# A transformer block in split fp32 on one Trainium2 core: dense passes read from the last token to the first, operands placed at other distances from the weights

## The reference, cut to what matters

```python
h = rms_norm(x, norm1_g); z = h @ w_in            # first block: four mixers on slices of z
x = x + mix @ w_out
hf = causal_dwconv(rms_norm(x, norm2_g) @ w_up, ffn_conv_w, ffn_conv_b)
gt, val = split(hf); x = x + (gelu(gt) * val) @ w_down
x = x + (p @ w_pe) * sigmoid(rms_norm(x, norm3_g) @ w_pg)
for l in range(2):                                 # second block, twice
    proj = (rms(x) * norm1_g) @ w_in               # attention, RWKV-7, retention, gates
    x = x + (g0 * o_a + g1 * o_b + g2 * o_c) @ w_out
    h2 = rms(x) * norm2_g
    x = x + (silu(h2 @ w_gate) * (h2 @ w_up)) @ w_down
```

## Time and profile before

| | |
|---|---|
| median of 3 runs | 2564.78 us |
| the profiled execution, its own time | 2564.04 us |
| its span, first to last instruction | 2562.2 us |
| TensorE busy | 2528.5 us, 99% of the span, 16344 matmuls |
| TensorE weight loads | 2012.7 us, 79% |
| GpSimd busy | 1510.1 us, 59% |
| VectorE busy | 1311.9 us, 51% |
| ScalarE busy | 691.3 us, 27% |
| mean granted TensorE clock | 0.998 of full |

### The profile page before, as it was taken

The page is one execution under the profiler, slowest core; times in us unless marked ns, Lnnn a source line. Parts: engine busy times, 40 slices in busy tenths (PEclk is TensorE's granted clock), DMA queues, the critical chain, the costliest instruction groups (busy, mean ns, idle before and its releaser), DMA issues.

```text
span 2562.2 us, 47105 instructions
## 1 busy us (share of the span) xinstructions
PE 2528.5 (99%) x16344; PEld 2012.7 (79%) x16344; DVE 1311.9 (51%) x1979; ACT 691.3 (27%) x1290; POOL 1510.1 (59%) x963
## 2 busy tenths in 40 slices
PE   8989999999999999999999999999999999999999
PEld 6868888887877778888888888877778888888887
DVE  7866555455566657763322224566547663322224
ACT  4452000034134446522100002135446521100002
POOL 5666666655646455556666666646455556666665
PEclk9999999999999999999999999999999999999999
DMA  4213222223211132223222223211132223222222
GB/s 166 71 46 115 94 95 98 92 84 116 98 44 52 43 100 73 72 79 103 99 93 96 98 92 120 91 51 52 43 98 71 69 85 103 92 97 98 91 97 99
DMA packets 72442, 222.55 MB, mean 87 GB/s; under 512 B 9312, under 2 KB 12256, under 8 KB 72288
## 3 DMA queue, kind: packets, MB, share of 16 engines
q1 hardware_dynamic: 71856, 220.36, 26.0%
q10 hardware_dynamic: 432, 0.14, 0.0%
HBM read 218.37 MB, written 2.10 MB: 86 GB/s over the span
## 4 chain that ended last, share of the span: by engine, by line
PE 93%; DVE 3%; DVEq 1%; DMA 1%; issue 1%; POOL 1%; ACT 0%; ACTq 0%; POOLq 0%; SPq 0%
PE acc L547 81%; PE bank L547 10%; DMA raw<-in_w_pg 1%; PE bank L1213 0%; POOL w_lo L377 0%; DVE y_lo L1251 0%; DVE sumsq L1251 0%; POOL w_hi L370 0%; DMA vec<-in_vec 0%; DVE xg_lo L1344 0%; DVE att L1463 0%; DVEq L1411 0%; DVEq L1708 0%; DVEq L1464 0%; DVE rw_kp L1732 0%
## 5 line engine op out<-in xcount | busy, mean ns | idle before, releaser
L377 POOL TENSOR_TENSOR w_lo<-raw,w_hi 128x1024 fp32r<-128x1024 f32 (+3 forms) x438 | 962.8, 2198 | 308.5 <-PE acc L547 246.0
L370 POOL TENSOR_SCALAR w_hi<-raw 128x1024 fp32r<-128x1024 f32 (+3 forms) x438 | 434.9, 993 | 596.1 <-PE acc L547 511.5
L547 PE MATMUL acc<-xg_hi,w_hi 128*128 128x512 f32 x2208 | 582.7, 398 | 6.1 <-DVE xg_lo L1344 3.2
L547 PE MATMUL acc<-xg_lo,w_hi 128*128 128x512 f32 x2208 | 569.0, 393 | 0.0
L547 PE MATMUL acc<-xg_hi,w_lo 128*128 128x512 f32 x2208 | 562.6, 393 | 0.2 <-POOL w_lo L377 0.2
L547 PEld LDWEIGHTS acc<-xg_hi,w_hi 128*128 128x128 f32 x2208 | 408.6, 188 | 107.6 <-issue 20.1
L547 PEld LDWEIGHTS acc<-xg_hi,w_lo 128*128 128x128 f32 x2208 | 411.4, 188 | 88.3 <-issue 1.5
L547 PEld LDWEIGHTS acc<-xg_lo,w_hi 128*128 128x128 f32 x2208 | 411.4, 188 | 87.5 <-issue 1.5
L2130 ACT ACTIVATE ffn_act<-ffn_t 128x512 f32<-128x512 f32 x100 | 63.3, 633 | 748.4 <-DVEq L1311 605.7
L1251 DVE TENSOR_TENSOR x<-x,acc 128x512 f32<-128x512 f32 x104 | 71.5, 688 | 323.5 <-PE acc L547 322.9
L1251 DVE TENSOR_TENSOR bank<-acc,rstd 128x512 f32<-128x512 f32 x72 | 50.4, 699 | 263.4 <-PE acc L547 263.2
(11 more groups left out here) (351 smaller groups left out, 2710.8 us busy)
## 6 DMA issues: line engine op xcount, KB each, us to landing
raw<-in_w_up SPq DMA_DIRECT2D x132, 512.0 KB, 3.2
raw<-in_w_down SPq DMA_DIRECT2D x48, 512.0 KB, 3.2
raw<-in_w_gate SPq DMA_DIRECT2D x48, 512.0 KB, 3.2
raw<-in_w_ret SPq DMA_DIRECT2D x32, 512.0 KB, 3.2
raw<-in_w_rw SPq DMA_DIRECT2D x28, 512.0 KB, 3.2
raw<-in_w_o SPq DMA_DIRECT2D x48, 256.0 KB, 2.7
raw<-in_w_in SPq DMA_DIRECT2D x18, 512.0 KB, 3.3
raw<-in_w_down SPq DMA_DIRECT2D x24, 384.0 KB, 3.0
```

Of the source, the lines that this page charges most:

```text
L370: nc.gpsimd.tensor_scalar(w_hi[:, s, 0:n], raw[:, s, 0:n], 1.0, 0.0, ALU.mult, ALU.add).then_inc(w_half[s], 1)
L377: nc.gpsimd.tensor_tensor(w_lo[:, s, 0:n], raw[:, s, 0:n], bits(w_hi[:, s, 0:n]), ALU.subtract).then_inc(w_split[s], 1)
L547: return nc.tensor.matmul(o, a, b, start=first, stop=last, skip_group_check=shared)
```

## The change

Every dense pass goes through a new helper `dense`, which hands `mm` its moving operand and its PSUM output with the token dimension reversed, both with step -1. Token t still meets output column t, and the weights are read as before. A helper `columns_of` names the weight slice. The small matmuls of the mixers, the norm sums (`stats`) and the transposes stay with `mm`.

The layout changes: `xg` stays at remainder 128 and the weights stay at 128. `raw` moves from 160 to 128, `rstd`, `sumsq` and what follows them by 32 bytes. The first block's `y` goes from 480 to 128, `emb` from 192 to 128, `z_rw` (whose space `y1` and `z_at` share) from 256 to 384. `z_rt` (whose space `y2` and `hid` share) stays at 256. So, with the weights at 128, the moving operands stand at distances 0 (`xg`, `y`, `emb`), 256 (`y1`) and 128 (`y2`, `hid`), where they were at 0 (`xg`), 352 (`y`), 64 (`emb`) and 128 (`y1`, `y2`, `hid`).

```diff
-WEIGHTS, OTHERS = 128, 160
+PLACE, PLACE_B1, PLACE_RT = 128, 384, 256
...
-        xg_hi, _ = place("xg_hi", (DC, T), F32R)
-        xg_lo, _ = place("xg_lo", (DC, T), F32R)
+        xg_hi, _ = place("xg_hi", (DC, T), F32R, line=PLACE)
+        xg_lo, _ = place("xg_lo", (DC, T), F32R, line=PLACE)
...
-        raw, _ = place("raw", (2, DC * P))
-        w_hi, _ = place("w_hi", (2, DC * P), F32R, line=WEIGHTS)
-        w_lo, _ = place("w_lo", (2, DC * P), F32R, line=WEIGHTS)
-        rstd, _ = place("rstd", (T,), line=OTHERS)
+        raw, _ = place("raw", (2, DC * P), line=PLACE)
+        w_hi, _ = place("w_hi", (2, DC * P), F32R)
+        w_lo, _ = place("w_lo", (2, DC * P), F32R)
+        rstd, _ = place("rstd", (T,))
...
-        y_hi, _ = place("y_hi", (DC, T), F32R)
-        y_lo, _ = place("y_lo", (DC, T), F32R)
+        y_hi, _ = place("y_hi", (DC, T), F32R, line=PLACE)
+        y_lo, _ = place("y_lo", (DC, T), F32R, line=PLACE)
...
-        z_rw, rw_at = place("z_rw", (14, T))
-        z_rt, rt_at = place("z_rt", (16, T))
+        z_rw, rw_at = place("z_rw", (14, T), line=PLACE_B1)
+        z_rt, rt_at = place("z_rt", (16, T), line=PLACE_RT)
...
-        emb_at = base + 24 * 1024
+        emb_at = base + 24 * 1024 + (PLACE - base) % LINE
...
+            def columns_of(w, s, k):
+
+                return w[:, s, k * P:(k + 1) * P]
...
+            def dense(o, a, b, first, last, shared=False):
+
+                return mm(o[:, ::-1], a, b[:, ::-1], first, last, shared)
...
                     for k, c in enumerate(chunks):
-                        last = mm(o[:], w[:, s, k * P:(k + 1) * P], v[:, c, :], v is hi and m == 0 and k == 0, m == 1 and k == n - 1)
+                        last = dense(o[:], columns_of(w, s, k), v[:, c, :], v is hi and m == 0 and k == 0, m == 1 and k == n - 1)
```

More of the change, by code:

```diff
@@ L582, in late @@
                     for k, c in enumerate(chunks[:-1]):
-                        w = slice(k * P, (k + 1) * P)
                         pe.wait_ge(ready, count + k + 1)
                         pe.sem_inc(pe_turn, 1)
-                        mm(acc[s][:], w_hi[:, s, w], a[0][:, c, :], k == 0, False)
-                        mm(acc[s][:], w_hi[:, s, w], a[1][:, c, :], False, False)
+                        dense(acc[s][:], columns_of(w_hi, s, k), a[0][:, c, :], k == 0, False)
+                        dense(acc[s][:], columns_of(w_hi, s, k), a[1][:, c, :], False, False)
                     pe.wait_ge(w_split[s], I + 2)
@@ L590, in late @@
                     for k, c in enumerate(chunks[:-1]):
-                        mm(acc[s][:], w_lo[:, s, k * P:(k + 1) * P], a[0][:, c, :], False, False)
+                        dense(acc[s][:], columns_of(w_lo, s, k), a[0][:, c, :], False, False)
                     if stat is not None:
@@ L595, in late @@
                     pe.sem_inc(pe_turn, 1)
[L596 to L599, removed]
+                    k, c = n - 1, chunks[-1]
+                    dense(acc[s][:], columns_of(w_hi, s, k), a[0][:, c, :], False, False)
+                    dense(acc[s][:], columns_of(w_hi, s, k), a[1][:, c, :], False, False).then_inc(hi_done[s], 1)
+                    dense(acc[s][:], columns_of(w_lo, s, k), a[0][:, c, :], False, True).then_inc(slot_done[s], 1)
                     return
                 for i, k in enumerate(order or range(n)):
-                    w, c = slice(k * P, (k + 1) * P), chunks[k]
+                    c = chunks[k]
                     pe.wait_ge(ready, count + i + 1)
                     pe.sem_inc(pe_turn, 1)
-                    mm(acc[s][:], w_hi[:, s, w], a[0][:, c, :], i == 0, False)
-                    last_hi = mm(acc[s][:], w_hi[:, s, w], a[1][:, c, :], False, False)
-                    last = mm(acc[s][:], w_lo[:, s, w], a[0][:, c, :], False, i == n - 1)
+                    dense(acc[s][:], columns_of(w_hi, s, k), a[0][:, c, :], i == 0, False)
+                    last_hi = dense(acc[s][:], columns_of(w_hi, s, k), a[1][:, c, :], False, False)
+                    last = dense(acc[s][:], columns_of(w_lo, s, k), a[0][:, c, :], False, i == n - 1)
                 last_hi.then_inc(hi_done[s], 1)
@@ L618, in three @@
             def three(s, a, k, first, last):
[L620 to L623, removed]
+                dense(acc[s][:], columns_of(w_hi, s, k), a[0][:, k, :], first, False)
+                hi_pass = dense(acc[s][:], columns_of(w_hi, s, k), a[1][:, k, :], False, False)
+                return hi_pass, dense(acc[s][:], columns_of(w_lo, s, k), a[0][:, k, :], False, last)
             def hid_slots(I, n, count, ahead=0):
@@ L815, in _ @@
             for c in full:
-                w = w_hi[:, 0, c * P:(c + 1) * P]
-                mm(acc[0][:], w, xg_hi[:, c, :], c == 0, False)
-                last = mm(acc[0][:], w, xg_lo[:, c, :], False, False)
+                w = columns_of(w_hi, 0, c)
+                dense(acc[0][:], w, xg_hi[:, c, :], c == 0, False)
+                last = dense(acc[0][:], w, xg_lo[:, c, :], False, False)
             last.then_inc(hi_done[0], 1)
@@ L821, in _ @@
             for c in full:
-                last = mm(acc[0][:], w_lo[:, 0, c * P:(c + 1) * P], xg_hi[:, c, :], False, c == DC - 1)
+                last = dense(acc[0][:], columns_of(w_lo, 0, c), xg_hi[:, c, :], False, c == DC - 1)
                 if c < DC - 1:
@@ L832, in one @@
                 def one(s, w, v, c, first=False, last=False):
-                    return mm(acc[s][:], w[:, s, c * P:(c + 1) * P], v[:, c, :], first, last, True)
+                    return dense(acc[s][:], columns_of(w, s, c), v[:, c, :], first, last, True)
                 def started(s):
@@ L887, in part @@
                         w, v, c = (w_hi, w_hi, w_lo)[k // DC], (xg_hi, xg_lo, xg_hi)[k // DC], k % DC
-                        last = mm(acc[s][:], w[:, s, c * P:(c + 1) * P], v[:, c, :], k == 0, k == 3 * DC - 1, True)
+                        last = dense(acc[s][:], columns_of(w, s, c), v[:, c, :], k == 0, k == 3 * DC - 1, True)
                         if k == 2 * DC - 1:
```

## The result

| | before | after |
|---|---|---|
| median | 2564.41 us (4 runs) | 2603.12 us (4 runs, 2601.37 to 2603.97) |
| ratio, 95% interval | | 1.015 [1.0132, 1.0168] |
| span of the profiled execution | 2562.2 us | 2600.8 us |
| TensorE busy | 2528.5 us | 2571.2 us |

The change makes the kernel slower by 38.7 us. The forecast was 2499 us.

A forecast was written before the change was run, and what follows sets the result against it. TensorE was taken to bound the kernel, its dense passes lengthened by two SBUF streams meeting. Savings of 36.0 + 2.3 + 18.6 + 7.7 = 64.6 us from 2564.0 us gave 2499 us, range 2445 to 2605.

The forecast's parts named there:

- step 3: Dense passes' PSUM output: writing the accumulator backwards costs 0 ns a pass.
- R3: Rival: the reversed PSUM write is slow, 429 ns a pass, about 4475 us in all; chance 0.03.
- I take half of each excess as gone: All dense passes: reversing the moving operand removes half the time above 214.5 ns, 6.1 ns per `xg` pass, 9.45 per `hid`.
- the prediction's floor of 214.5 ns: Dense pass with nothing in its way, read from the fp32 record as two streams of 512 columns, 214.5 ns each.
- the term of `xg`: `xg` passes, 6.1 ns less each: 36.0 us saved outside the RWKV gaps and 2.3 us as filler.
- R2: Rival: distance 0 suits forward order only; reversed `xg` loses 6.7 ns a pass, 2609 us, or 2627 with others; chance 0.22.
- R1: Rival: `xg`'s 12.2 ns excess is a fixed cost per fp32r pass, whatever the order; 2545 or 2564 us; chance 0.25.
- Step 2: New distances: first block's `y` and `emb` at 0 gain 1.6 us forward, `y1` at 256 between -2.5 us and 0.
- The filler: 768 `xg` passes in the RWKV stretches: 4.7 us saved, half counted, 2.3 us, since shorter filler partly becomes longer waits.

The follow-up runs named there:

- scan_quiet: Dense passes alone, no block computed; read and write reversed separately at 64 distances: at distance 0, 226.7 ns a pass read forward, 233.3 read reversed.
- the scans: Three kernels of dense passes alone, no block computed, varying reading order, distance, address and columns; 331 to 763 us.
- step 0: In a kernel of dense passes alone, the moving operand reads one value over and over: 215.7 to 215.9 ns a pass at all eight distances.
- zero_fwd: Kernel after the change, but read forward and with every moving operand at distance 0 from the weights: 2547.45 us, ratio 0.9932 to before.

## Why the prediction was wrong

**The frame held.** TensorE bounds the kernel, a pass's time from start to start is the quantity, and its change shows in the time: the spans differ by 38.6 us, the sums of starts by the same. No other engine came in, the 32-byte moves cost nothing that shows, and the backward write is free, as costed in step 3; R3 fell by scan_quiet.

**The step that failed** is the first, "I take half of each excess as gone". It took 6.1 ns off each `xg` pass and 9.45 off each `hid` pass. Measured, the reversal adds to both: over the prediction's floor of 214.5 ns, `xg`'s excess goes from 12.2 to 18.8 and `hid`'s from 18.9 to 22.1, and the term of `xg`, put at -38.3 us, came out at +35.4. The sign was wrong. I argued that since placement changes a third of the excess, reversing would act on the rest. But that placement matters said nothing on which way another order goes, and "that it suits a reversed stream is an estimate" was the link on which nearly all of the 64.6 us hung. Forward at distance 0 was already a best case: no distance of the scans gives less than its 226.7 ns by more than rounding. From a best case a new order is more likely to leave than to improve; that should have turned the chances toward R2.

The time of 2603 us lies inside the stated range only since that was drawn up to 2605 to hold half of R2; the forecast of a faster kernel gets nothing from it.

**R2** had the right price and half the right reason. It gave 2609 us from `xg` going to `hid`'s 233.4, and `xg` went to 233.3. That the sum comes so near is in part luck: it is 9 us too high for the passes in short rows and leaves out the 4.8 us of `hid`. And it supposed that reversed order has a good distance elsewhere; there is none. R1, the fixed cost, fell with step 0 at 215.7 ns. The Trainium skill's sentence "PE and ACT never wait on anyone", with its independent read ports for the moving operand and the weights (SBUF — State Buffer, "Who interferes with whom"), was taken under R1 to mean that order and distance change nothing. Taken so, it isn't borne out: by order and distance alone the same pass takes 226.7 or 233.3 ns here, with all other engines idle. The Trainium skill's rule on patterns that aren't contiguous (Advanced Engine Details and Errata, "PSUM Cachelines"), weighed under R3, doesn't reach a step of -1: six passes that wrote backwards took the same 1.52 us as six that wrote forward.

**Step 2** was right that `y` and `emb` gain at distance 0 in forward order, and put `y1` at 256 between nothing and 2.5 us; it is the full gain, since 256 is as good as 0. The floor that I took from the fp32 record, 214.5 ns, was nearly right; the lowest pass measured takes 215.7.

**The filler** was costed at half of its change. It is rather more than a third: 0.8 us for 2.1 in one of the two stretches. The reason given, that TensorE's waits there take up part of any change, shows little: it is idle for 4.8 of 230 us before and for 4.5 of 230 us after. What is missing are passes that weren't at 226.7 to begin with.

**What stays open.** Shown is that the excess needs a moving operand that walks through fp32r data (215.7 ns with step 0), that forward it is about constant for each pass from 256 to 512 columns, and that, with a new weight chunk for each pass, it depends on the order of the 16-byte groups and on the distance modulo 256. Argued only is that the two streams collide in SBUF, and that the price goes with the weight load. The order in which the array takes the weights is in no row, and a reversed weight read wasn't measured. Step 0 on the weights left most of the excess, which a plain count of colliding addresses doesn't explain, and neither does the good distance of 240 with a repeated weight chunk.

## What to carry to other kernels

For rows of fp32r passes of 128x512, each with another weight chunk, put every moving operand a multiple of 256 bytes from the weights, all on multiples of 32 bytes, and read it forward: 226.7 ns a pass instead of 229 to 240, and 0.7% of this kernel by placement alone (zero_fwd). In rows of a few passes between small matmuls expect little of it. Measure such an effect with a scan of passes alone before costing it: three short kernels of 331 to 763 us gave the map, which reasoning from four placements hadn't. When an observed case may already be the best point of a curve that isn't known, give the other side more weight than the room that seems left.

## What the runs showed of the hardware that was not expected

- After a jump to other addresses up to some ten passes are needed to settle at 226.7, even between groups that are both at distance 0. With both operands moved by 64 bytes, the first eight of 24 passes took 230, 224, 231, 236, 228, 232, 231 and 227 ns, and then 226 to 227 for the rest. Inside the block a row that begins after small matmuls shows the same start (233.0 ns in its second pass, 227.4 in its eleventh); from slot to slot within a row none is seen.
- bf16 passes of the same size take 215.8 ns in either order at 0, 128, 256 and 384 bytes, so this is a matter of fp32r. Whether the moving bytes or the weights free them isn't told apart: their weight loads are shorter too, 98 ns for 188.
- 192 columns take 111.7 ns in both orders, 31.7 over their columns, where 256 columns take 120.0 forward. What sets that pace isn't shown.
